# Reordering weight units in a two-layer streaming encoder step: dense, dense, modulation, modulation instead of taking turns

## The reference

```
def ada_modulation(c, w, b):
    mod = jax.nn.silu(c) @ w + b               # w: 2048 x 12288 for each layer
    return [m[:, None, :] for m in jnp.split(mod, N_MOD, axis=-1)]
...
h = rms_norm(x, g_mix[i]) * (1.0 + scale1) + shift1
...                                            # layer 0: qkv, stick-breaking attention, w_o
x = x + gate1 * mix                            # layer 1: pooling mixer
h = rms_norm(x, g_ffn[i]) * (1.0 + scale2) + shift2
x = x + gate2 * swiglu(h, w_gate[i], w_up[i], w_down[i])     # D_FF = 5632
```

## Time and profile before

| | us |
|---|---|
| runs of the kernel before | 3421.37, 3413.59, 3415.03 |
| median | 3415.03 |
| span of the profiled execution | 3414.0 |
| TensorE busy in the span | 3265.0 (96%) |
| VectorE busy | 2119.0 (62%) |
| ScalarE busy | 1309.1 (38%) |
| GpSimd busy | 137.6 (4%) |

### The profile page before, as it was taken

The page is one execution under the profiler, slowest core; times in us unless marked ns, Lnnn a source line. Parts: engine busy times, 40 slices in busy tenths (PEclk is TensorE's granted clock), DMA queues, the critical chain, the costliest instruction groups (busy, mean ns, idle before and its releaser), DMA issues.

```text
span 3414.0 us, 47966 instructions
## 1 busy us (share of the span) xinstructions
PE 3265.0 (96%) x20219; PEld 2953.3 (87%) x20219; DVE 2119.0 (62%) x1855; ACT 1309.1 (38%) x994; POOL 137.6 (4%) x124
## 2 busy tenths in 40 slices
PE   7999998889989999999999999769999999999999
PEld 3677776667979999999999999659999999999999
DVE  4488885567887777777776777784344443344443
ACT  3344444455453343334433443443223222322221
POOL 0000000000000000000000000110000000000000
PEclk9999999999999999999999999889999999999999
DMA  9777777877645555556555565544343333333331
GB/s 352 269 263 248 249 244 251 304 278 263 231 160 185 199 206 185 193 176 210 205 177 192 184 209 197 190 158 145 123 131 127 123 124 133 125 123 124 127 130 62
DMA packets 325816, 646.49 MB, mean 189 GB/s; under 512 B 10881, under 2 KB 13513, under 8 KB 325321
## 3 DMA queue, kind: packets, MB, share of 16 engines
q1 hardware_dynamic: 317144, 630.17, 54.1%
q10 hardware_dynamic: 8586, 15.09, 1.3%
HBM read 631.46 MB, written 14.74 MB: 189 GB/s over the span
## 4 chain that ended last, share of the span: by engine, by line
PE 88%; DVE 5%; DMA 4%; ACT 2%; issue 1%; POOL 0%; SPq 0%; ACTq 0%; DVEq 0%; POOLq 0%
PE bank L1511 23%; PE bank L1513 23%; PE bank L1512 23%; PE bank L1595 3%; PE bank L1538 3%; PE bank L1597 3%; PE bank L1596 3%; DMA raw<-in_w_ada 2%; PE bank L1701 1%; DMA raw<-in_cache_v 1%; PE bank L1523 1%; PE bank L1742 1%; DVE w_lo L956 0%; PE bank L1547 0%; DMA early_raw<-in_w_qkv 0%
## 5 line engine op out<-in xcount | busy, mean ns | idle before, releaser
L956 DVE TENSOR_TENSOR w_lo<-raw,w_hi 128x2048 fp32r<-128x2048 f32 x323 | 738.9, 2290 | 877.7 <-ACT w_hi L569 877.7
L569 ACT ACTIVATE w_hi<-raw 128x2048 fp32r<-128x2048 f32 x323 | 616.3, 1915 | 1352.4 <-PE bank L1513 1168.7
L1511 PE MATMUL bank<-h_hi,w_hi 128*128 128x384 f32 x3136 | 1063.9, 339 | 34.3 <-DVE h_lo L1042 24.1
L1512 PE MATMUL bank<-h_lo,w_hi 128*128 128x384 f32 x3136 | 1052.2, 336 | 0.0
L1513 PE MATMUL bank<-h_hi,w_lo 128*128 128x384 f32 x3120 | 1047.7, 336 | 0.0
L1511 PEld LDWEIGHTS bank<-h_hi,w_hi 128*128 128x128 f32 x3136 | 591.9, 189 | 79.3 <-issue 67.1
L1512 PEld LDWEIGHTS bank<-h_lo,w_hi 128*128 128x128 f32 x3136 | 592.3, 189 | 0.0
L1513 PEld LDWEIGHTS bank<-h_hi,w_lo 128*128 128x128 f32 x3120 | 589.0, 189 | 0.0
L1511 PE MATMUL bank<-act_hi,w_hi 128*128 128x384 f32 x1408 | 472.9, 336 | 0.0
L1513 PE MATMUL bank<-act_hi,w_lo 128*128 128x384 f32 x1408 | 470.6, 334 | 0.0
L1512 PE MATMUL bank<-act_lo,w_hi 128*128 128x384 f32 x1408 | 470.5, 334 | 0.0
(11 more groups left out here) (231 smaller groups left out, 2501.5 us busy)
## 6 DMA issues: line engine op xcount, KB each, us to landing
raw<-in_w_ada SPq DMA_DIRECT2D x192, 1024.0 KB, 5.8
raw<-in_w_gate SPq DMA_DIRECT2D x88, 1024.0 KB, 5.2
raw<-in_w_up SPq DMA_DIRECT2D x88, 1024.0 KB, 5.2
raw<-in_w_down SPq DMA_DIRECT2D x88, 1024.0 KB, 5.1
raw<-in_w_qkv SPq DMA_DIRECT2D x40, 1024.0 KB, 5.2
raw<-in_cache_k SPq DMA_DIRECT2D x32, 1024.0 KB, 6.0
raw<-in_cache_v SPq DMA_DIRECT2D x32, 1024.0 KB, 7.2
raw<-in_w_o SPq DMA_DIRECT2D x15, 1024.0 KB, 5.1
```

The source lines that it names most:

```text
L569: act.activation(w_hi[:, s], raw[:, s], ACT.Copy).then_inc(hi_ready, 1)
L956: dve.tensor_tensor(w_lo[:, s], raw[:, s], w_hi[:, s].bitcast(f32), ALU.subtract).then_inc(lo_ready, 1)
L1511: pe.matmul(out, w, a, start=start, stop=False)
L1512: pe.matmul(out, w, al, start=False, stop=False)
```

## The change

In QKV, the output projection and the first feed-forward the units of a block are ordered dense, dense, modulation, modulation, and so again. Every engine's program and the load queue follow. With it come:
- `norm_apply` on VectorE (norms 1 and 3): both next pieces are scaled and the first of them split before any weight unit, then units 2, 3 and 4 stand between the later pieces. In norm 1 the last `mod_in` of the output projection moves in, after the second split; unit 1, now dense, stands between `square_sum` and `norm_root`.
- In QKV the head norms of block n - 1 move on VectorE from the end of their own block to between the units 4 to 7 of block n; ScalarE issues the stores of heads after unit 8 instead of after unit 6.
- In the output projection VectorE adds to the residual once the sixth unit is done (before: the seventh), with units 9 to 11 after it.
- In the feed-forward TensorE's order of the up half is d8, the transposes, d9, m10, m11, d12, d13, m14, m15; ScalarE takes the gate half once unit 5 is done (before: unit 6). The first chunk of both feed-forwards is written out ahead of the loop on ScalarE and VectorE, since unit 4 is already made in the norm.
- The waits of SyncE's queue at the end of QKV stand as they were, but the sixth unit there is now the last dense one.

```
+        def turns(n):
+            return n % 4 >= 2, 2 * (n // 4 % 2) + n % 2
...
             def mixed(W, n):
                 W, s = unit(W, n)
-                if n % 2:
+                if turns(n)[0]:
...
             def norm_apply(n, W):          # VectorE
                 norm_scale(n, 2, 2, 2)
                 norm_split(n, 0, 2, 1, half_ready)
                 norm_split(n, 2, 2, 2)
-                for g in range(1, 4):
-                    if g >= 2:
-                        dve.wait_ge(h_ready, HR[n] + g - 1)
-                    norm_scale(n, 4 * g, 4, g + 2)
-                    for s in BETWEEN[n][g]:
-                        (mixed if n == 1 else dense)(W, s)
-                    if g >= 2:
-                        norm_split(n, 4 * g - 4, 4, g + 1)
+                put = mixed if n == 1 else dense
+                if n == 1:
+                    mod_in(ADA_O + 3, other_half(3))
+                norm_scale(n, 4, 4, 3)
+                dve.wait_ge(h_ready, HR[n] + 1)
+                norm_scale(n, 8, 4, 4)
+                norm_split(n, 4, 4, 3)
+                put(W, 2)
+                norm_split(n, 8, 4, 4)
+                put(W, 3); put(W, 4)
+                dve.wait_ge(h_ready, HR[n] + 2)
+                norm_scale(n, 12, 4, 5)
                 norm_split(n, 12, 4, 5)
...
             def qkv_block(n, last):        # VectorE
+                late = n > EARLY and n % 3
                 mixed(W, 4)
                 if n > EARLY:
                     mod_in(ADA_QKV + n - EARLY - 1, 7)
+                if late:
+                    head_vars(n - 1)
                 mixed(W, 5)
+                if late:
+                    head_gain(n - 1)
+                mixed(W, 6)
                 if n % 3:
                     head_scale(n - 1)
-                mixed(W, 6); mixed(W, 7)
+                mixed(W, 7)
                 if not last:
-                    mixed(W, 8); mixed(W, 9); mixed(W, 10)
-                if n % 3 < 2:
-                    head_vars(n)
-                if not last:
-                    mixed(W, 11)
-                if n % 3 < 2:
-                    head_gain(n)
+                    for u in range(8, 12):
+                        mixed(W, u)
...
             def qkv_block(n):              # TensorE
-                for j in range(4):
-                    to_tokens(W, 2 * j, qkv_half(n), j)
-                    if j == 0 and n > EARLY:
-                        ada_turn(a - 1, 7)
...
-                    ada_sub(W, 2 * j + 1, a, j, 6)
+                to_tokens(W, 0, qkv_half(n), 0)
+                if n > EARLY:
+                    ada_turn(a - 1, 7)
...
+                to_tokens(W, 1, qkv_half(n), 1)
+                ada_sub(W, 2, a, 0, 6)
+                ada_sub(W, 3, a, 1, 6)
+                to_tokens(W, 4, qkv_half(n), 2)
+                to_tokens(W, 5, qkv_half(n), 3)
+                ada_sub(W, 6, a, 2, 6)
+                ada_sub(W, 7, a, 3, 6)
...
             # output projection, VectorE
-                dve.wait_ge(sub_used, 4 * W + 7)
+                dve.wait_ge(sub_used, 4 * W + 6)
...
-            mod_in(ADA_O + 3, other_half(3))
             norm_coef(1)
             square_sum(1, 3)
+            mixed(W_FFN0, 1)
             norm_root(1)
             norm_apply(1, W_FFN0)
```

More of the change, by code:

```diff
@@ L355, in _, with load_eight @@
             load_early(7)
-            def load_pair(W, j, dense, layer, a):
-                for n, src in ((2 * j, dense), (2 * j + 1, ada_src(layer, a, j))):
-                    load(*unit(W, n), src)
+            def load_eight(W, dense, layer, a, start=0):
+                for n in range(start, 8):
+                    ada, j = turns(n)
+                    load(*unit(W, n), ada_src(layer, a, j) if ada else dense(j))
             def qkv_rows(n, j):
@@ L448, in load_mixed @@
                 for i, w in enumerate((w_gate, w_up)):
-                    for j in range(4):
-                        load_pair(W + 2 * i, j, rows(w[0, j * 512:(j + 1) * 512, ds(c * 512, 512)]), layer, a + i)
+                    load_eight(W + 2 * i, lambda j: rows(w[0, j * 512:(j + 1) * 512, ds(c * 512, 512)]), layer, a + i)
                 load_down(W + 4, 0, c)
@@ L871, in mixed_chunk, with dense_chunk @@
                         square_last(2)
-            def dense_chunk(W, c, last=False):
-                for n in range(4, 7):
+            def dense_chunk(W, c, first=False, last=False):
+                for n in range(5 if first else 4, 7):
                     dense(W, n)
@@ L933, in _ @@
             norm_apply(3, W_FFN1)
-            with act.Fori(0, CHUNKS - 1) as c:
+            dense_chunk(W_FFN1, CHUNKS, first=True)
+            with act.Fori(1, CHUNKS - 1) as c:
                 dense_chunk(W_FFN1 + c * 3, c + CHUNKS)
@@ L1410, in rows_out, with dense_chunk @@
                     dve.tensor_copy(yrow[:, t, q * 512:(q + 1) * 512], bank[:, y_bank(q) + t]).then_inc(y_dve, 1)
-            def dense_chunk(W, c, r, last=False):
-                for n in range(4, 11):
+            def dense_chunk(W, c, r, first=False, last=False):
+                for n in range(5 if first else 4, 11):
                     dense(W, n)
@@ L1423, in dense_chunk @@
                         rows_out(s)
-            with loop(dve, 0, CHUNKS - 1, {step: 4 * ADD + 2}) as c:
+            mixed_chunk(W_FFN0, 0, ADA_FFN, 0, R_FFN0, mixed, first=True)
+            with loop(dve, 1, CHUNKS - 1, {step: 4 * ADD + 2}) as c:
                 mixed_chunk(W_FFN0 + c * 5, c, ADA_FFN + c * 2, 0, R_FFN0 + c * 4, mixed)
@@ L1499, in _ @@
             norm_apply(3, W_FFN1)
-            with loop(dve, 0, CHUNKS - 1, {step: 4 * ADD}) as c:
+            dense_chunk(W_FFN1, CHUNKS, R_FFN1, first=True)
+            with loop(dve, 1, CHUNKS - 1, {step: 4 * ADD}) as c:
                 dense_chunk(W_FFN1 + c * 3, c + CHUNKS, R_FFN1 + c * 4)
@@ L1812, in _ @@
                 for j in range(4):
+                    n = (0, 1, 4, 5)[j]
                     if i == 0 and j == 3:
```

110 lines of the change are left out of this document (57 added, 53 removed).

## The result

The changed kernel takes 3391.18 us (median of 4 runs, 3388.93 to 3393.24) against 3414.36 of the kernel before (4 runs, 3413.59 to 3421.37): a ratio of 0.9927, 95% interval 0.9915 to 0.9939. The forecast was 3387.5 with a range of 3376 to 3403, so the direction and the range hold and the forecast is 3.7 us too low. The profiled execution took 3390.14 us with a span of 3388.4 us; the prediction had 3386.5 for the span.

A forecast was written before the change was run, and what follows sets the result against it. TensorE was taken as the bound, busy 3265.0 of 3414.0 us. The terms -6.3, +2.0, -2.8, -2.4, -13.3 and -4.7 sum to -27.5: span 3386.5, time 3387.5, range 3376 to 3403.

The forecast's parts named there:

- The rhythm: TensorE's dense and modulation units: two modulation units side by side save 0.33 us per pair, over 72 pairs.
- The rival that the gap belongs to the unit: Modulation pairs on TensorE: the 0.33 us belongs to each unit, so pairs save nothing; time 3410, chance 0.08.
- VectorE in QKV: QKV blocks: VectorE keeps up, with a slack of 0.4 us at unit 8 in six blocks, costing nothing.
- the other side: First feed-forward: two modulation units hold VectorE, making the dense unit behind late in every chunk; 3437 at worst, chance 0.05.
- The first block: First QKV block: its first pair gains nothing, since a 2.58 us wait ends at 176.87 in either order.
- Into attention: From QKV to attention: q and k loads wait for the later sixth unit, adding 2.0 us.
- The upper bound, 5: From QKV to attention: the added time is at most 5 us, with a lowered clock.
- Output projection: Output projection: pairs save 2.0 us in blocks 0 to 2 and 1.35 in block 3, less 0.6; sum -2.8.
- Norm 1 and chunk 0: Norm 1 into the first feed-forward chunk: the 3.80 us wait goes, VectorE pays part back; -2.4 us with two pairs.
- bare wait until 28.1: Norm 1: VectorE, after a scaling ending at 25.9 us, waits for ScalarE until 28.1, counted from TensorE's d0.
- Norm 3: Norm 3: the 3.11 us wait and 1.5 of half clock go, less 0.1 of restart; -4.7 us.
- the 1.0 that was taken between span and time: Whole kernel: 1.0 us added to the forecast span of 3386.5 to reach the median of 3387.5.

The follow-up runs named there:

- units_only: The changed kernel's new unit order, but VectorE and ScalarE in norms 1 and 3 in the order of the kernel before; 3402.89 us, ratio 0.9966.
- after_again: The changed kernel measured once more, unchanged; 3393.55 us, ratio 0.9934 against the kernel before.
- v_late: The changed kernel, but the first v load for attention waits until the last QKV block's v stores have landed; 3392.19 us, ratio 0.9929.
- last_old: The changed kernel, but the last QKV block alone keeps the old order of units; 3390.87 us, ratio 0.993.
- q_early_v_late: The changed kernel with attention's first query load issued earlier, after d4 of the last QKV block, and the v load after the v stores; 3391.8 us.
- unit5_in: The changed kernel, but in norm 1 unit 5's weights are made before the last token tiles are rounded and split; 3391.94 us, ratio 0.9929.
- last_old_v_late: The changed kernel with the old unit order in the last QKV block and the v load after the v stores; 3389.45 us, ratio 0.9922.

## Why the prediction was right, and what was mis-sized

**The rhythm.** Right. A pair saves 0.317 in QKV ((297.18 - 292.11) / 16 over eight blocks) and 0.333 in the chunks ((1088.13 - 1074.80) / 40, with units_only's and after_again's 1074.80; the first profile of the changed kernel has 1074.40), 0.33 predicted. The rival that the gap belongs to the unit is out. The Trainium skill, TensorEngine Tiling (Array Packing), Key Properties, has a change of tiling mode drain TensorE. The trace agrees in that a second unit of the same mode adds no gap (1.45 us for the pair). That the mode is the reason is not shown: the two kinds also differ in type, float32 and bf16, and no run separates the two.

**VectorE in QKV.** Right, and close. In the block whose d0 starts at 341.45, VectorE ends unit 8 at 375.21 + 2.29 = 377.50 and TensorE wants it at 377.96: a slack of 0.46, 0.4 predicted.

```profile
375.21 2.29 DVE L962 TENSOR_TENSOR w_lo<-raw,w_hi 128x2048 fp32r<-128x2048 f32 x1
...
377.96 0.50 PE L1605 MATMUL bank<-w_hi,h_hi 128*128 128x512 f32 x1
```

No wait came in 8 blocks. In the chunks unit 12 is ready at 1237.38 and wanted at 1240.56, 3.2 us, where 3.1 was predicted; the mechanism of the other side never comes near.

**The first block.** One wait was predicted to stay, 2.58 at 176.87. It became 1.43 before m3 and 1.35 before d4, and the total is the same within 0.2 us; d4 starts 21.0 us after d0 in both kernels, as predicted. What the working left out is the clock behind it: the granted clock was 0.51 from 176.87 to 180.00 before and is 1.00 after, worth an estimated 1.5 us (3.13 us at half speed). Less these 0.2 and a start of the block that was 0.5 later, it makes the -7.0 of QKV out of the -6.3.

**Into attention.** This is the term that was mis-sized: +2.0 was predicted with kT at M + 8.7 to 10.3, and it came at M + 13.1, +5.6 from E. The places were named rightly (loads behind d5, the v load with them, a new wait for a DMA before the transposes). Both of its paths were priced too low. The end of the v stores was taken at M + 7.5 from the old profile. The last of them took 3.5 us before (533.49 to 537.02) and 9.2 now (526.51 to 535.67), and it is what kT waited for last, at M + 13.1. The working noted that the stores share the traffic but put no price on it. The other path, from the loads over the transposes, was put at M + 8.7 to 10.3 and measures M + 12.5. The last k load landed at M + 8.5 and not at M + 7 to 8, since its 6.1 to 7.0 us came from a stretch in which the v load was not yet out. And the transposes before kT, put at 2.1 us, took 3.9, because the lowered clock stood in the bounds and not in the value. The upper bound, 5, was exceeded. The runs show what each edit gives: 2.5 from holding back the v load (v_late), 3.5 from the old order of the last block (last_old), and 3.5 to 4.0 from both, so most of it is shared. No edit removed the lowered clock: all 24 transposes took 1.3 to 2.6 us longer than before in every kernel with the new order, also where the last block kept the old one. Where kT waited for the stores, this was not on its path. Which share each transfer has in the others' delay was not tried.

The Trainium skill, DMA: Bandwidth & Descriptors, Anatomy of one DMA, gave an estimated landing of M + 6 from its fixed cost and a full queue; it has that cost for transfers issued from GpSimd, and these are SyncE's. The transposes that wait for the landing began at M + 8.6. With the v load held back they began at M + 6.9 (v_late), and at M + 6.3 in q_early_v_late, where only the k tiles are issued late.

**Output projection.** -2.8 predicted, -2.6 measured, with the 0.6 for unit 1 before norm_root in it. Block 0's wait, put at about 0.5, is 1.35 us (819.87, before d4).

**Norm 1 and chunk 0.** Right by its steps. Predicted from P: m3 waits to 20.6, d4 for 22.9, d5 for 32.4, d8 at 43.65. Measured: 20.45, 22.66, 32.09 and 43.35. The 3.80 wait was traded for four of 3.95 in all, so the gain is not in the waits: -2.9 from P to chunk 0's last result against -2.4. It comes from the cheaper pairs and from the clock, which was 0.54 after the old wait (985.33 to 987.33) and is 1.00 after the new ones (986.25 to 988.25). The waits left before d5 and d8 come from the order of VectorE's work and not from its amount, as the working implied with its bare wait until 28.1; unit5_in shows it by 2.2 us.

**Norm 3.** -4.7 predicted. From P to the last residual add it is 1109.24 before (3405.01) and 1104.73 after (3378.85), -4.5. d1 starts without a wait, and the window that had 0.50 has 1.00:

```profile
2274.12 0.68 PE L1521 MATMUL bank<-h_hi,w_hi 128*128 128x384 f32 x1 [8.66 <-DVE h_lo L1048]
...
2288.35:2290.35 2.00, 2.00 (x14) 2.00 (x13) 2.00 (x2) 0.00 (x0) 0.00 (x0) 1.00 0.66 256
```

**Not in the sum.** About 2.3 us was lost where nothing was changed. The two sums of norm 2 and those of norm 3 take 1.65 us each time instead of 0.91, and the last transposes of the span 2.82 instead of 1.99, all at a lower clock (0.50; before 1.00, 1.00 and 0.73) behind a wait of nearly the same length as before (3.53, 3.18 for 3.10, and 3.08). The profile after has the first and the last so:

```profile
2156.60 1.65 PE L1565 MATMUL bank<-nbuf,ones 128*128 128x384 f32 x2 [3.53 <-DVE nbuf L1011]
...
3381.89 2.82 PE L1915 MATMUL bank<-ident,x 128*128 128x128 f32 x12 [3.08 <-DVE x L1085]
```

What shifted the clock there is open. The last transposes take 2.67 to 2.82 us in all eleven kernels with the new norms and 1.99 and 2.03 in the two without; the sums take now 0.91 and now 1.32 to 1.65, in no relation to an edit that the profiles show.

**The total.** Of the 3.7 us between forecast and median, 1.9 lie in the span. Another 0.7 lie in the 1.0 that was taken between span and time: every execution on record has 1.7 to 1.9 there. The last 1.0 is the distance of this profiled run from the median. That the total came so close has luck in it. The way to kT cost 3.6 us more than forecast, QKV gave 0.7 more and the first feed-forward 1.0 more, and the rest of attention drew 264.2 us, near the short end of its scatter; after_again, the same kernel, took 3393.55.

## What to carry to other kernels

- Where TensorE alternates between two shapes of matmul, count the changes of shape and not the units; here a pair put side by side saved 0.32 to 0.33 us, read over 56 of the 72 pairs; where waits decide, in norm 1, the engine that prepares the weights needs the matching order too. One half of such a change can be worth nothing or less in a stage (norm 1: +3.0 with the units alone, +0.7 with the norms alone, -3.3 with both).
- When a step's trigger moves later, price its transfers with everything that will then be in flight beside them, and also those that it slows: here the stores that nobody had moved ended last. Let the engine that waits pay at the lower clock. Where an idle time is shortened only in part, the clock can keep the gain.
- Stages read from anchors in the traces resolved edits of 2 us that medians over five runs, with a scatter of 5 us, did not.

## What was not expected of the hardware

- 24 token transposes took 2.81 us after a wait of 1.20, and 5.38 us at a granted clock of 0.50 after one of 2.22 (before and last_old_v_late, both with four transposes and a wait of 0.7 ahead). Longer waits did not make it worse in order: 5.74 was followed by 4.58 us, since the clock rose to full while they ran, and 6.24 in the same kernel once more by 5.38; 2.34 was followed by 4.51. So in these runs the length of the wait alone does not say what the clock costs.
- The same last v store, issued the same 2.4 us after E, needed 3.5 us before, when the q and k loads were over and the v load nearly so, and 9.2 us with these in flight.
- In last_old the last k load was out by 521.64, at E - 5.2, and the transposes could start only at 530.44, 8.8 us later, behind the loads of cache_k; in v_late, issued after them, the last was out by 526.87 and they started at 532.17, 5.3 us later.
